# A channel mixer on TensorE, paced by the gathered rows that VectorE works through beside it

## The reference

```python
# first block, per token t: 8 heads x 16 chosen experts = 128 rows of each table
u = expert_u[eidx]; v = expert_v[eidx]
act = gelu(einsum('td,thkd->thk', xb, u))
ff  = einsum('thk,thkd->td', g * act, v)
...
# second block
y = square(relu(h2 @ w_up)) @ w_down        # 1024 -> 4096 -> 1024
x = x + rmsnorm_2(y, post_norm_mlp)
```

## Time and profile before

| | us |
|---|---|
| runs shown | 3034.2 median of three (3020.66, 3034.2, 3040.07) |
| the profiled execution | 3046.39, of which span 3044.7 |
| TensorE busy in the span | 2399.5 (79%) |
| VectorE busy | 1750.0 (57%) |
| GpSimd busy | 1205.8 (40%) |
| the stage `mlp` for three tiles | 2308.0 to 2771.3 in the span |

### The profile page before, as it was taken

How to read it: one execution, slowest core, us unless ns; L and a number is a source line. 1 busy time by engine, 2 the same in 40 slices (tenths; PEclk the granted TensorE clock), 3 DMA queues, 4 the chain that set the end, 5 groups by cost and what they waited for, 6 DMA issues and landing times. The chain is left out here.

```text
span 3044.7 us, 28171 instructions
## 1 busy us (share of the span) xinstructions
PE 2399.5 (79%) x9768; PEld 1676.8 (55%) x9768; DVE 1750.0 (57%) x3620; ACT 574.6 (19%) x1560; POOL 1205.8 (40%) x1058
## 2 busy tenths in 40 slices
PE   6988899889747866997786854865787725999888
PEld 5847788565634544885553632443664312556755
DVE  3315410279998886477777759668767795000410
ACT  4411300112322220001112012311232000112221
POOL 0000000005886666476554856765646572000000
PEclk9998999999978987999998966987878857999989
DMA  3331233338999999799978988998988996243366
GB/s 143 139 117 49 93 142 139 131 142 358 414 353 354 363 359 405 296 417 418 354 276 300 354 350 299 353 346 351 415 340 342 382 410 240 103 161 114 136 231 246
DMA packets 173228, 832.05 MB, mean 273 GB/s; under 512 B 20880, under 2 KB 21136, under 8 KB 156192
## 3 DMA queue, kind: packets, MB, share of 16 engines
q0 software_dynamic: 147456, 536.94, 46.2%
q1 hardware_dynamic: 25632, 293.33, 24.6%
HBM read 828.09 MB, written 2.10 MB: 273 GB/s over the span
## 5 line engine op out<-in xcount | busy, mean ns | idle before, releaser
L1192 POOL DMA_INDIRECT expert_rows<-in_peer_u,chosen x512 | 661.5, 1292 | 1041.0 <-DVE chosen L1763 672.0
L1192 POOL DMA_INDIRECT expert_rows<-in_peer_v,chosen x512 | 540.9, 1056 | 285.1 <-issue 147.4
L1266 DVE SCALAR_TENSOR_TENSOR expert_rows<-expert_rows,u 128x1024 f32<-128x1024 f32 x512 | 602.7, 1221 | 62.6 <-DMA expert_rows<-in_peer_u,chosen 35.0
L2900 PE MATMUL mlp_up<-mlp_xT,mlp_slab 128*128 128x384 f32 (+1 forms) x1024 | 249.1, 401 | 92.2 <-issue 65.5
L1226 PE MATMUL expert_sum<-expert_rows,expert_diag 128*128 128x512 f32 x496 | 246.6, 644 | 33.5 <-ACT expert_diag L1213 25.4
L2900 PEld LDWEIGHTS mlp_up<-mlp_xT,mlp_slab 128*128 128x128 f32 x1024 | 163.8, 200 | 183.5 <-issue 99.0
L1276 DVE SCALAR_TENSOR_TENSOR h<-expert_rows,expert_coef,h 128x1024 f32<-128x1024 f32 x194 | 251.5, 1296 | 10.7 <-DMA expert_rows<-in_peer_v,chosen 5.1
L1276 DVE SCALAR_TENSOR_TENSOR u<-expert_rows,expert_coef,u 128x1024 f32<-128x1024 f32 x190 | 246.4, 1297 | 9.7 <-DMA expert_rows<-in_peer_v,chosen 7.4
L691 PE MATMUL product<-uT,in_slab 128*128 128x272 f32 (+1 forms) x1024 | 238.1, 388 | 8.1 <-DMA in_slab<-in_w_in 8.1
L2891 PE MATMUL mlp_down<-mlp_slab,upT 128*128 128x512 f32 x512 | 227.1, 599 | 17.1 <-issue 17.1
L691 PEld LDWEIGHTS product<-uT,in_slab 128*128 128x128 f32 x1024 | 192.3, 192 | 39.4 <-issue 8.6
(11 more groups left out here) (543 smaller groups left out, 3220.2 us busy)
## 6 DMA issues: line engine op xcount, KB each, us to landing
in_slab<-in_w_in SPq DMA_DIRECT2D x34, 2048.0 KB, 7.7
mix_slab<-in_w_in SPq DMA_DIRECT2D x16, 2048.0 KB, 8.4
mlp_slab<-in_w_up SPq DMA_DIRECT2D x16, 2048.0 KB, 8.5
mlp_slab<-in_w_down SPq DMA_DIRECT2D x16, 2048.0 KB, 7.6
expert_rows<-in_w_in SPq DMA_DIRECT2D x9, 2048.0 KB, 7.6
mix_slab<-in_ssd_w_out SPq DMA_DIRECT2D x8, 2048.0 KB, 8.3
out_slab<-in_w_out SPq DMA_DIRECT2D x6, 2048.0 KB, 7.9
mix_slab<-in_sc_w_out SPq DMA_DIRECT2D x4, 2048.0 KB, 8.7
```

Source lines behind the costliest of these rows:

```text
L1192: pool.indirect_dma_start(out=self.row(n), out_offset=None, in_=self.tables[0 if dot else 1], in_offset=bass.IndirectOffsetOnAxis(ap=picks ...
L1266: dve.scalar_tensor_tensor(self.row(n), self.row(n), 1.0, u, ALU.mult, ALU.mult, accum_out=dot).then_inc(self.rows_used, 1)
L2900: ins = pe.matmul(bank[n % UPS][:, 0:W], slab[i % R][:, k, j * P:(j + 1) * P], xT[:, k, :], start=k == 0, stop=k == KD - 1)
```

## The change

In the stage with row units, each of TensorE's slabs i = 1 to 7 waits until i eighths of the stage's units are used by VectorE: with 171 units that is 21, 42, 64, 85, 106, 128 and 149. Slab 0 and slabs 8 to 15 get no wait. The gelu moves one place ahead in ScalarE's order, from before group n = 9 to before n = 8. The call for the last tile, which has no `bg`, gets neither.

```diff
-    GELU_AT = 9
+    GELU_AT = 8
+
+    paced = range(1, 8) if bg else ()
+    rows_at = [(bg.goal - bg.base) * i // 8 if i in paced else 0 for i in range(2 * COUNT)]
...
+                if i in paced:
+                    pe.wait_ge(bg.rows_used, bg.by_vector(bg.base + rows_at[i]))
                 pe.wait_ge(landed[i % R], 16 * (i // R + 1))
```

## The result

The changed kernel took 3066.9 us, the median of 14 runs, and the kernel before, run beside it, 3035.2: a ratio of 1.0102, with a 95% interval of 1.008 to 1.0124. So it is 1% slower, where I had forecast 50 us faster. Its profiled execution has a span of 3055.7 us. One thing has to be known for all that follows: in five of the seven later sittings (a sitting is one series of executions, of before and of others beside it, on one chip) the kernel before took only 2824 to 2829 us, and in two 3038 and 3046 us.

What follows compares the result with a forecast made beforehand. TensorE was taken to bound the stage, slowed beside unbroken gathers. Slab 7 starting at 2528.5 would end the stage 56 us sooner; less 6 for slow records, 3034.2 - 50 = 2984 us, own range 2970 to 3004 (8 in 10: 2970 to 3062).

Steps and rivals of the forecast that it cites:

- What bounds the kernel: In the changed stage TensorE sets the end; it lost 133 us ahead of 2584, with idle time labelled "issue".
- Does TensorE keep the pace?: Slabs 1 to 7: TensorE manages a slab per 31 us, as loads break up the gathers; 6 us lost at slab 7.
- the slow pace: TensorE in the stage: one matmul record in 2.8 us, going with long unbroken runs of gathers beside TensorE at full rate.
- The seven waits: Slabs 1 to 7: slab 1 starts at 2332, slab 2 at 2367, losing 18 us of full-rate time; waits themselves cost 0.
- When rows end: End of the stage's row units: 2556.7 instead of 2552.5 if TensorE keeps the pace; slab 7's unit 149 at 2528.5.
- the other case: Rows' end if the slow pace catches slab 2: four loads instead of six, rows end at 2536.
- The first rival: The slow pace catches slab 2 and stays: stage ends 17 to 32 us later, 3051 to 3066 us; chance 0.24.
- point of decision: The first rival decides the outcome if TensorE has done fewer than some 220 records by 2521; forecast nearly 400.
- The clock: Half clock after each rest: some 3 us per slab, inside 10 us of slack; rival of lasting half rate, 3022, chance 0.07.
- Direct gain 0: The GELU one place ahead ends the rows 6 us sooner, but rows do not set the end, so it gains 0.
- the stop it took away: The late GELU stopped the gathers for 17 us and so freed TensorE at 2380; losing this counts against the change.
- The gelu follows the last dot by 2 us: Sign of a right forecast: ScalarE's gelu comes 2 us after VectorE's last dot, where VectorE had waited 22.2 us.

Runs made afterwards that it cites:

- after_again: The changed kernel unchanged, run again in a sitting with the slow pace; 1.0064 of the kernel before.
- after_c: The changed kernel unchanged, its third timing, in a sitting with the slow pace; ratio 1.0032 to the kernel before.
- after: The changed kernel with all its parts, as profiled in the first comparison with the kernel before; median 3066.9 us, ratio 1.0102.
- after_e: The changed kernel unchanged, in a sitting without the slow pace; stage 408.0 us, against 330.5 with the GELU move alone.
- waits12: The changed kernel with only the waits of slabs 1 and 2 and the GELU at its old place; 16.6 us of stage lost.
- before_again: The kernel before, unchanged, run for its trace in a sitting with the slow pace; its mixer stage took 452.7 us.
- gelu_only: The kernel before with only the GELU one place ahead and no waits; no change in time, in a sitting without the slow pace.
- graded_b: Repeat of the kernel before with the stage's gathers paced in four parts, in a sitting with the slow pace; 3.8% faster than before.
- gelu_only_e: Repeat of the kernel before with only the GELU one place ahead, in a sitting without the slow pace; stage 330.5 us.
- graded: The kernel before with gathers paced in four parts: as before, two sizes of fill, then at most 6 units ahead; no cost without the slow pace.
- pause4: The kernel before with a GpSimd fill of 512 columns ahead of each gather of the stage; 1.3% slower without the slow pace.
- waits37: The changed kernel with only the waits of slabs 3 to 7, GELU ahead; 2.4% slower than before, without the slow pace.

## Why the prediction was wrong

**What bounds the kernel.** The prediction has it right for this execution: TensorE sets the end, it loses 133 us, at 2.8 us a record. But I took the loss for a property of the kernel. In five of seven later sittings it isn't there at all, with the same program. One profile and three times within 0.7% of each other gave no hint of it.

**The step that failed** is "Does TensorE keep the pace? ... I take the second, because its cause is likelier to hold". It has two halves. Where the slow pace is there, TensorE kept ahead of the rows only up to slab 3: rests of 3.3, 6.1 and 9.9 us, with slabs 24, 30 and 40 us apart, did not hold the slow pace off, nor did 14.7 and 17.3 us ahead of slab 3 in after_again and after_c. Slab 4's rows were done at 2415.7 in after, and it started at 2532.49. The cause that I counted on was that slabs' loads break the run of gathers; a load is issued only when SyncE hears that a slab is done, and it heard it 18 and then 87 us late. Four loads fell into the rows, not eight. Where the slow pace is not there, TensorE kept ahead of the rows in all seven slabs (after_e), and the waits had nothing to cure.

**The seven waits.** Slabs 1 and 2 were forecast at 2332 and 2367 in before's time, 24 and 59 us into the stage; measured 24.2 and 53.9, and 24.6 and 52.5 in after_e. The second came 5 to 6 us sooner than forecast. "TensorE loses 18 us of time in which it ran at full rate" was too much by a third: slab 2 started 12.5 us later than before's 41.4. (waits12 lost 16.6 us of stage, with 13.8 of them at slab 2's start and the rest by the clock.)

**When rows end.** Forecast 2556.7 - 2308 = 249 us into the stage if TensorE keeps the pace: 247 in after_e. For the other case 228: 230 in after. Both right. So was the whole timetable of a TensorE that keeps the pace: slab 7 at 220.5 and the end at 407.1 us, against 218.9 and 408.6 in after_e. Only there before needs 331 us, not 463, and what was to be a gain of 56 us is a loss of 77.

**The first rival** is what happened in the comparison. It gave slab 2 slow throughout, rows ending at 228 us, 183 records when TensorE recovers, slab 7 late, 3051 to 3066 us from the median of 3034. Measured: slab 2 slow only in its last third, then slab 3; rows at 230; 208 records at 2511; the stage 22 us longer, inside its 17 to 32. The median of 3066.9 us lies at the top of its range, though, and the profiled execution of 3057.4 us is near its middle only because the stage began 12.7 us sooner, which nobody forecast. Its point of decision, 220 records, stands. I gave it 0.24 by the argument that the rests speak against it. They don't. The size varies: the profiled stages of after_again and after_c are 21.8 and 21.4 us longer than that of before_again, but their ratios are 1.0064 and 1.0032.

**The clock.** 3 us per rest were forecast, and 2.6 to 3.2 were measured in after_e. "Inside the 10 us of slack" was wrong where there is no slow pace, since there it stands on the path together with the waits.

**The GELU.** Direct gain 0: right, five times, without the slow pace. That the stop it took away counts against the change where the slow pace is there was not tried alone: gelu_only met no such sitting. In its favour, TensorE came free with the stop in before, before_again, after_again and graded_b; in after the ring was full for only 3.4 us, at 2365, ahead of all of the slow pace. But the rows' end came 6 to 15 us sooner in the stage with the change as well, and the waits put slabs 1 to 3 back. "The gelu follows the last dot by 2 us" failed in after: it came 13 us after it, behind the relu of slab 1's last group, which ran at 2361.19. In after_e it came at once. How the 22 us divide among these stays open.

**What stays open.** What makes the sittings differ. It is not the program and not the chip's number. The gaps of 2.8 us (52 in before), with shorter ones of 1.4 and 2.1 us beside them (38 and 19), and the updates that are late by a growing time look like a full queue behind TensorE. The Trainium skill (NOTIFIC — the notification-queue block, section 7.1) says that the path that carries an engine's records away can stall the engine when a queue is full; that would be an effect of recording an execution. Every time here comes with a span and a granted clock from a recording, so no run shows what the kernel takes without one.

The packed traces speak for this rival. In the sittings without the slow pace, those of the kernels of 28171 instructions hold 25,110 to 25,115 records of semaphore updates each; where the slow pace is there, before and the changed kernel, of as many instructions, hold 17,043 to 17,628. A third of the records is missing, most of them of landing DMAs (11,977 left in before, 19,216 in gelu_only_e). Between 100 and 230 us into the stage seven eighths are missing (187 in before, 1472 in gelu_only_e), and in its first 60 us, while TensorE still ran at full rate, already a third (416 and 666). In graded_b, between 100 and 230 us, where no slow pace came, there are 1319, and 1390 in graded. So lost records and slow pace go together; which of them brings the other, or what brings both, is not shown. Density against backlog, and a fixed fill against a shorter queue, were not told apart either.

## What to carry to other kernels

Before curing a stall that one profile shows, ask for a second sitting of the same kernel: a loss that no instruction explains ("issue", "remote") may belong to the sitting, and a cure by waits then costs its full length where the loss is absent, here 2.8% against a hoped 1.6%. Read the late engine through those who wait for it: the time from a record to its reader, 18 us here, is the first sign. Count the trace's own records too: a third fewer semaphore updates from the same program shows that the recording lost some, and then the loss of time may be the recording's too. Doubt the label "issue" where a wait was added: two of the three waits for rows stood under it. If a background stream disturbs the engine on the path, pace the stream, which had slack, and not the engine, which had none; graded gained 3.8% where the trouble was, while pause4, whose stream ended too late, lost 1.3 to 1.4% where it wasn't.

## What the hardware showed unexpectedly

The same program on the chip of the same number took 2825 us at one time and 3046 at another, each time steady within 1.2%. In the slower sittings TensorE's updates reached ScalarE and SyncE up to 88 us late while gathers ran 1.2 to 1.3 us apart. In the others equally dense gathers did no harm as far as they went: from 2315 to 2332 us waits37 had 14 gathers at 409 GB/s, and TensorE did 49 records, busy for all 17 us; from 2250 to 2326 us gelu_only_e had 57 at 416 GB/s, and TensorE did 205 records, busy for all 76 us. The traces of the slower sittings lack a third of the semaphore updates. After a rest of TensorE of 3.7 us the granted clock was 0.50 for the next 5.7 us.
